# The second feed-forward's gate and up products: three 256-column matmuls per weight tile instead of one of 512 columns and one of 256

## What is computed

```python
hs = hs + 0.5 * swiglu(rmsnorm(hs, ffn1_norm), w_gate1, w_up1, w_down1)      # 2048 -> 5632 -> 2048
hs = hs + token_mixing(rmsnorm(hs, mix_norm), w_in, ..., w_out)              # causal convolutions
hs = hs + 0.5 * swiglu(rmsnorm(hs, ffn2_norm), w_gate2, w_up2, w_down2)
out = rmsnorm(hs, final_norm)[:, 16:]
swiglu(h, g, u, d) = (silu(h @ g) * (h @ u)) @ d
```

## Time and profile before

| | value |
|---|---|
| median of 3 runs | 1873.63 us |
| the profiled execution's own time | 1873.27 us |
| its span, first to last instruction | 1871.5 us |
| PE busy | 1860.6 us (99%) |
| DVE busy | 1111.8 us (59%) |
| ACT busy | 922.2 us (49%) |
| mean share of the 16 DMA engines in their main queue | 57.3% |
| granted TensorE clock | 0.999 of full speed |
| gu2 on PE | 1130.84 to 1619.39 us |

### The profile page before, as it was taken

The page is one execution under the profiler, slowest core; times in us unless marked ns, Lnnn a source line. Parts: engine busy times, 40 slices in busy tenths (PEclk is TensorE's granted clock), DMA queues, the critical chain, the costliest instruction groups (busy, mean ns, idle before and its releaser), DMA issues.

```text
span 1871.5 us, 32101 instructions
## 1 busy us (share of the span) xinstructions
PE 1860.6 (99%) x13017; PEld 1760.0 (94%) x13017; DVE 1111.8 (59%) x1218; ACT 922.2 (49%) x1173; POOL 5.9 (0%) x17
## 2 busy tenths in 40 slices
PE   9999999999999999999999999999999999999998
PEld 9999999999999999999999998888888888888886
DVE  7555555555554545468899887555566655544444
ACT  6434334344343444359888665444444444444443
POOL 1000000000000000000000000000000000000000
PEclk9999999999999999999999999999999999999999
DMA  6655555555555555555655565665555666665654
GB/s 224 194 174 177 171 179 172 175 178 171 178 174 176 179 173 178 177 172 170 189 184 181 169 202 187 190 189 188 190 180 188 191 194 193 207 196 190 194 189 134
DMA packets 283357, 342.26 MB, mean 183 GB/s; under 512 B 10639, under 2 KB 223985, under 8 KB 283152
## 3 DMA queue, kind: packets, MB, share of 16 engines
q1 hardware_dynamic: 282672, 340.44, 57.3%
q10 hardware_dynamic: 320, 0.53, 0.1%
q0 software_dynamic: 288, 0.19, 0.0%
HBM read 339.02 MB, written 2.10 MB: 182 GB/s over the span
## 4 chain that ended last, share of the span: by engine, by line
PE 99%; DVE 1%; ACT 0%; issue 0%; DVEq 0%
PE ps L466 20%; PE ps L467 20%; PE ps L468 20%; PE ps L473 17%; PE ps L474 9%; PE ps L569 4%; PE ps L567 4%; PE ps L568 4%; PE ps L448 0%; DVE w_lo L886 0%; PE ps L428 0%; PE ps L585 0%; DVE zc L1098 0%; PE ps L591 0%; DVE ln_mu L912 0%; PE ps L488 0%
## 5 line engine op out<-in xcount | busy, mean ns | idle before, releaser
L886 DVE TENSOR_TENSOR w_lo<-raw,w_hi 128x1024 fp32r<-128x1024 f32 x639 | 781.3, 1224 | 653.0 <-ACT w_hi L650 647.7
L650 ACT ACTIVATE w_hi<-raw 128x1024 fp32r<-128x1024 f32 x639 | 675.6, 1058 | 845.0 <-PE ps L468 508.7
L466 PE MATMUL ps<-x_hi,w_hi 128*128 128x272 f32 (+2 forms) x2048 | 588.5, 287 | 1.2 <-DVE x_lo L895 1.2
L467 PE MATMUL ps<-x_lo,w_hi 128*128 128x272 f32 (+2 forms) x2048 | 587.6, 287 | 0.0
L468 PE MATMUL ps<-x_hi,w_lo 128*128 128x272 f32 (+2 forms) x2048 | 583.9, 285 | 0.0
L473 PE MATMUL ps<-x_both,w_hi 128*128 128x512 f32 x1408 | 488.4, 392 | 0.0
L474 PE MATMUL ps<-x_both,w_lo 128*128 128x256 f32 x1408 | 394.4, 280 | 0.0
L467 PEld LDWEIGHTS ps<-x_lo,w_hi 128*128 128x128 f32 x2048 | 386.6, 189 | 0.1
L466 PEld LDWEIGHTS ps<-x_hi,w_hi 128*128 128x128 f32 x2048 | 384.8, 188 | 1.5 <-DVE w_lo L1120 1.4
L468 PEld LDWEIGHTS ps<-x_hi,w_lo 128*128 128x128 f32 x2048 | 385.7, 188 | 0.0
L473 PEld LDWEIGHTS ps<-x_both,w_hi 128*128 128x128 f32 x1408 | 263.4, 187 | 57.6
(11 more groups left out here) (148 smaller groups left out, 1148.3 us busy)
## 6 DMA issues: line engine op xcount, KB each, us to landing
raw<-in_ffn_w_up SPq DMA_DIRECT2D x176, 512.0 KB, 3.5
raw<-in_ffn_w_down SPq DMA_DIRECT2D x176, 512.0 KB, 3.7
raw<-in_ffn_w_gate SPq DMA_DIRECT2D x175, 512.0 KB, 4.1
raw<-in_w_in SPq DMA_DIRECT2D x80, 512.0 KB, 3.4
raw<-in_w_out SPq DMA_DIRECT2D x32, 512.0 KB, 4.6
x_tok<-in_x SPq DMA_DIRECT2D x4, 512.0 KB, 7.5
gain_tok<-in_final_norm SPq DMA_DIRECT2D x1, 1024.0 KB, 7.0
out_y<-o_tok SPq DMA_DIRECT2D x2, 512.0 KB, 2.9
```

Source lines behind the costliest of these rows:

```text
L466: pe.matmul(dst, w_high, act_high, start=first, stop=False)
L467: pe.matmul(dst, w_high, act_low, start=False, stop=False)
L650: act.activation(w_hi[s][:, :], raw[s][:, :], ACT.Copy).then_inc(hi_ready, 1)
L886: dve.tensor_tensor(w_lo[s][:, :], raw[s][:, :], w_hi[s][:, :].bitcast(F32), ALU.subtract).then_inc(lo_ready, 1)
```

## The change

Gu2 goes back to the form of the other stages. `wide_product`, the buffer `gu2_lo` and the two semaphores around it go; gu2 uses `product` with rows of 256 columns and gu1's eviction. `x2_both` becomes `x2_hi` and `x2_lo`, which lie one behind the other and begin 192 bytes into their region. The mixer's buffers begin 192 bytes into theirs, not 64.

```diff
-        x2_both = at("x2_both", x_at, [P, 2, KD, SEQ], F32R)
+        x2_hi = at("x2_hi", x_at + 192, [P, KD, SEQ], F32R)
+        x2_lo = at("x2_lo", x_at + 192 + 4 * KD * SEQ, [P, KD, SEQ], F32R)
...
-        gu2_lo = at("gu2_lo", a_at + 4 * 2 * KF * SEQ, [P, SET, SEQ])
...
-        mix_at = a_at + 64
+        mix_at = a_at + 192
...
-                                if phase == "gu2":
-                                    m = wide_product(bank, w_hi[s][:, cols], w_lo[s][:, cols],
-                                                     x2_both[:, :, k, :], x2_both[:, 0, k, :],
-                                                     k == 0, k == KD - 1)
-                                else:
-                                    m = product(bank, width[phase], w_hi[s][:, cols], w_lo[s][:, cols],
-                                                x_hi[:, k, toks], x_lo[:, k, toks], k == 0, k == KD - 1)
+                                moving = ((x2_hi[:, k, :], x2_lo[:, k, :]) if phase == "gu2"
+                                          else (x_hi[:, k, toks], x_lo[:, k, toks]))
+                                m = product(bank, width[phase], w_hi[s][:, cols], w_lo[s][:, cols],
+                                            *moving, k == 0, k == KD - 1)
...
-                if phase == "gu2" and at_step == 0:
-                    bank = SET * ((g if isinstance(g, int) else parity_of[0]) % 2)
-                    act.wait_ge(block_used, before_block(phase, g, n_blocks[phase]))
-                    act.activation(gu2_lo[:, :, :], ps[:, bank:bank + SET, SEQ:2 * SEQ],
-                                   ACT.Copy).then_inc(low_copied[phase], 1)
...
-                        if phase == "gu2":
-                            act.wait_ge(scaled["gu2"], g + 1)
-                        else:
-                            act.wait_ge(emptied, read + 2)
+                        act.wait_ge(emptied, read + 2)
                         act.activation(t1[:, :, 0:w], t1[:, :, 0:w], ACT.Silu).then_inc(silu_ready[phase], 1)
...
-                if phase == "gu2" and at_step == 0:
-                    u = t12[:, :, 0:SEQ]
-                    dve.wait_ge(low_copied["gu2"], g + 1)
-                    dve.tensor_tensor(u, ps[:, bank:bank + SET, 0:SEQ], gu2_lo[:, :, :],
-                                      ALU.add).then_inc(emptied, SET)
-                    dve.wait_ge(emptied, read + SET)
-                    dve.tensor_tensor(u, u, over_two(rstd[:, toks], SEQ, SET),
-                                      ALU.mult).then_inc(scaled["gu2"], 1)
-                if phase in ("gu1", "ag", "cv"):
+                if phase in ("gu1", "ag", "cv", "gu2"):
```

More of the change, by code:

```diff
@@ L133, in build @@
                 "gu2": (a2_both[:, 0, :, :], a2_both[:, 1, :, :])}
-        gu2_lo = at("gu2_lo", a_at + 4 * 2 * KF * SEQ, [P, SET, SEQ])
-        assert SET * SEQ <= 2 * KF * (T - SEQ)
         x_tok = at("x_tok", a_at, [P, HALVES, D])
@@ L211, in build @@
         sc_first = sem("sc_first")
-        low_copied, scaled = {"gu2": sem("low_copied_gu2")}, {"gu2": sem("scaled_gu2")}
         gain_spread, tile_done = sem("gain_spread"), sem("tile_done")
@@ L468, in product @@
                 return pe.matmul(dst, w_low, act_high, start=False, stop=last)
[L470 to L474, removed]
             def start_group(phase, g):
@@ L656, in operand @@
                 act.wait_ge(emptied, 2 * (t // 2) + 2 if norm == "start" else banks_before(norm, 0) + t + 1)
-                dst = x2_both[:, 0, t, :] if phase == "gu2" else x_hi[:, t, toks]
+                dst = x2_hi[:, t, :] if phase == "gu2" else x_hi[:, t, toks]
                 act.activation(dst, res[:, t, toks], ACT.Copy,
@@ L833, in _ @@
             act.wait_ge(par_ready, 4)
-            parity_of = [0]
             def phase_blocks(phase, norm=None, between=None):
                 def body(g, parity):
-                    parity_of[0] = 1 - parity
                     for i in range(n_blocks[phase]):
@@ L892, in operand @@
                 dve.wait_ge(xhi_ready[norm], t + 1)
-                high, low_part = ((x2_both[:, b, t, :] if phase == "gu2" else (x_hi, x_lo)[b][:, t, toks])
-                                  for b in (0, 1))
+                high, low_part = ((x2_hi[:, t, :], x2_lo[:, t, :]) if phase == "gu2"
+                                  else (x_hi[:, t, toks], x_lo[:, t, toks]))
                 dve.scalar_tensor_tensor(low_part, res[:, t, toks], param(gain_of[norm], t),
@@ L953, in finish @@
                         dve.wait_ge(silu_ready[phase], g + 1)
[L954 to L957, removed]
+                        dve.wait_ge(emptied, read + 4)
                         dve.tensor_tensor(t2[:, :, 0:w], t1[:, :, 0:w], t2[:, :, 0:w],
```

## The result

The changed kernel takes 1880.05 us (median of 6 runs, 1879.73 to 1882.15) against 1873.56 for the kernel before in the same comparison: ratio 1.0036, 95% interval 1.0023 to 1.0049. The change makes the kernel slower by 6.5 us where 9.3 were forecast; the predicted time was 1882.7.

The account below looks back on a forecast made before the run. PE's matmul stream was taken to bound the kernel: 1873.27 us profiled plus 9.3 us in gu2, mixer and eviction at 0, gave 1882.6, stated as 1882.7 us. Likeliest range 1879 to 1886, wider range 1870 to 1889.

Parts of the forecast that it names:

- PE's start-to-start distance sets gu2's time; ACT, DVE and DMA have room: Gu2's time is its matmul count times the distance between starts; nothing else moves the end unless it starves PE.
- The price of a tile now, 346.7 ns: In gu2 with wide matmuls, 488.55 us less 0.44 for the norm's sum, over 1408 tiles.
- The price after, 353.3 ns, from rows that start at 64: Gu2's new tile price, taken from the output stages' three 256-column matmuls: +9.3 us, range +7.2 to +12.0.
- The mixer's move at 0: 256 output-stage tiles, rows moved from 64 to 192: nothing; likely -0.4 to +0.5 us, outer bounds -3.4 to +4.3.
- a price other than 352 to 355 ns: Sign of being wrong, in gu2 or the output stages: the start 192 would be the cause, both moving together.
- Eviction at 0: Gu2's evictions: 23.7 us less DVE work and 22.3 less on ACT, hidden under PE, so 0 us.
- rival 4: The eviction was holding PE somewhere and its removal pays; no size, given no weight of its own.
- Rival 2: Start 192 is fast in gu2 and mixer: 342 ns per tile, -6.6 and -2.9 us, 1863.8 us; chance 0.15.
- Rival 1: Splitting is cheap at a single start: gu2 tile 348 to 349 ns, about 1875 to 1877 us; chance 0.12.
- Rival 3: Start 192 is bad in gu2 and mixer: 360 ns per tile, +20.4 us, 1893.7 us; chance 0.10.

Follow-up runs that it names:

- sum_twice: The changed kernel with the norm's sum in gu2 issued twice in a row, no wait added: 1862.02 us, and 1862.08 us over 6 runs when timed again.
- stall_once: The changed kernel with one added wait of PE in gu2's first group, two blocks after the norm's sum: 1863.33 us (5 runs).

## Why the prediction was right, and where not

1. *PE's start-to-start distance sets gu2's time; ACT, DVE and DMA have room.* Right. No idle time of PE appeared, and 24.3 us less work on DVE bought nothing.
2. *The price of a tile now, 346.7 ns.* Right for the profiled execution. It is one of two paces of the kernel before; in the other (353.3, 1882.8 us) the change would have been a gain of 2.8 us. Nothing in one execution could show that.
3. *The price after, 353.3 ns, from rows that start at 64.* Right in number: 497.50 us against 497.9. But the reason given, that the start hardly matters in the mean, was wrong. The price by start runs from 340.0 to 360.0, and 353.3 came out because the norm's sum leaves the stream in the slower of the two paces of 192, which happens to be the price of rows at 64. So the hit was luck. Without the sum's effect the same change would have ended near 1862, as sum_twice did.
4. *The mixer's move at 0.* This is the term that was mis-sized: -2.5 us, so that the sum was 2.5 us too high. Its outer bound (-3.4) held it, its likely range (-0.4 to +0.5) did not. The prediction named a price other than 352 to 355 ns in the output stages as a sign of being wrong, and 340.0 is such a price; that gu2 and the output stages would then move together did not come true.
5. *Eviction at 0.* Right, so rival 4 is out. The two multiplications out of PSUM take 692 and 680 ns in gu2 against the 687 taken; DVE's wait for ACT is gone.
6. *Rival 2, the start 192 is a good one.* Held at 0.15, with 114 ns per matmul and 342 per tile. It is a true mechanism: it measured 340.0 in most of the output stages and in 32 tiles of gu2, and 1863.3 us in stall_once against the 1863.8 worked out for it. That this agrees to 0.5 us is partly chance: the pace is 2 ns below the 342 assumed, and the stall and the tiles that run at 353.3 all the same make up for part of it. What spoke against it, that short and long distances cancel within a stage, held only for rows that walk through the starts. Stage b, cv and ag walk, and their means of 353 to 375 ns say nothing on a row of one start. A mean over positions was used as the price of one position.
7. *Rivals 1 and 3.* Rival 1 is out: rows at 0 in the split form take 360.0 ns, the most of all. The 0.115 us after the w_lo matmul was part of the wide pair's rhythm. Its own terms also add up to 1874 to 1876 us, 1 us less than it was given: +1.8 to +3.2 in gu2 and -1.4 to -1.1 in the mixer. Rival 3's 360 ns exist, but at the start 0; at 192 no run showed them.

The Trainium skill (TensorE: Matmul & The Clock Gate, section Back-to-back issue gap) gives the distance between matmuls as a function of the number of columns alone. These runs disagree: the same three matmuls of 256 columns take 340.0 to 360.0 ns as their rows' start changes, and 340.0 or 353.3 at one start.

Shown is: which starts have which pace, that one sum moves a stream at 192 from 340.0 to 353.3, that a stall brings it back and a second sum leaves it at 340.0, and that the pace then holds for 1359 tiles and more. Only argued is why: that the stream of weight loads and that of moving rows meet in SBUF or in the array at a fixed distance, which a disturbance resets. Open is why the kernel before has either pace from one execution to the next, while the two wide kernels with the mixer at 192 and the split ones seldom or never changed theirs, and what the heap at 1871.8 us and the single runs 2 us above the others are; none of them was profiled. A uniform start for the 272-column rows of the earlier stages wasn't run, nor was the split form of gu2 at 64 or 128.

## What to carry to other kernels

Where TensorE is the bound, price a matmul stream by start-to-start distances of the same shape and the same operand starts, count the tiles between two starts, and look for a change of pace inside a stage: the printed busy time (99% in all cases here) hides the 4% between 340.0 and 353.3. Try the few starts modulo 256 bytes of both operands, one size at a time. And when an experiment or a kernel's runs fall into heaps whose difference is the same few nanoseconds for every tile of a stage, take the disturbance before the stage (an odd matmul, a stall) as a knob of its own.

## What was not expected of the hardware

- A stream of three float32r matmuls of 256 columns, with a weight load each and all rows at 192 modulo 256, has two steady paces: 340.0 and 353.3 ns at the full granted clock (0.999), which are 16 and 26.7 array cycles of 2.4 GHz per matmul above its 256.
- The pace is a memory. One float32 matmul pair turned 340.0 into 353.3 for the 1375 tiles left; 1.21 us of idle time brought 340.0 back, and with a second pair the stream went on at 340.0, both to the stage's end.
- The moving rows' start modulo 256 bytes is worth up to 20 ns per tile (6%; 340.0 at 192, 360.0 at 0), and that of the stationary rows up to 6.5 ns per 512-column matmul (0 against 64).
- One compiled kernel without any change has execution times 9.3 us apart at the same granted clock (0.998 or 0.999). In the two executions that were profiled, 9.37 of 9.75 us are one stage's matmul pace.
